# Two loads and one wait moved at the tail of the down projection: the last tile's weights issued before two operand loads, and the residual rows read back without waiting for the last split

## The reference, cut to what matters

```
g_, u_ = split(f @ w_gate_up)                 # (544 x 1024) @ (1024 x 5632)
hid    = silu(g_) * u_                        # 544 x 2816
x      = x + rmsnorm(hid @ w_down, g_ffn_post)  # w_down 2816 x 1024; x here is x1, the residual
```

## Time and profile before

| | us |
|---|---|
| Median of three runs | 766.47 |
| The profiled execution's own time | 765.87 |
| Its span, first to last instruction | 764.1 |
| TensorE busy (matmuls) | 753.5, 99% of the span |
| VectorE busy | 519.1, 68% |
| ScalarE busy | 376.5, 49% |
| GpSimd busy | 124.1, 16% |

### The profile page before, as it was taken

One profiled execution on the slowest core, in us unless ns is written; L12 is line 12 of the kernel. 1 busy time (PEld: TensorE's weight loads), 2 busy tenths in 40 slices (PEclk: granted clock), 3 DMA queues, 4 the chain that ended last, 5 costly groups with the idle time before them and its releaser, 6 DMA issues.

```text
span 764.1 us, 16113 instructions
## 1 busy us (share of the span) xinstructions
PE 753.5 (99%) x5909; PEld 713.0 (93%) x5909; DVE 519.1 (68%) x822; ACT 376.5 (49%) x670; POOL 124.1 (16%) x240
## 2 busy tenths in 40 slices
PE   8999999999999999999999999999999999999995
PEld 6988899898898899987899999999999999999995
DVE  7556838647666565784469887778777899665543
ACT  7334625634634642343456555545555468444441
POOL 6602102010120110012000000000000000373553
PEclk9999999999999999999999999999999999999998
DMA  9545546545554225525470333322333112433273
GB/s 259 167 111 119 152 115 139 154 106 125 136 130 105 73 60 169 165 79 178 158 207 12 111 110 110 107 83 85 110 110 109 56 49 84 136 93 110 71 219 133
DMA packets 183097, 91.77 MB, mean 120 GB/s; under 512 B 50358, under 2 KB 175754, under 8 KB 183052
## 3 DMA queue, kind: packets, MB, share of 16 engines
q1 hardware_dynamic: 176606, 82.41, 39.1%
q0 software_dynamic: 5264, 8.41, 3.9%
q10 hardware_dynamic: 1182, 0.35, 0.2%
HBM read 82.37 MB, written 6.81 MB: 117 GB/s over the span
## 4 chain that ended last, share of the span: by engine, by line
PE 93%; POOL 3%; DMA 2%; DVE 1%; issue 1%; DVEq 0%; SPq 0%; POOLq 0%; ACT 0%
PE ps L1079 34%; PE ps L1468 28%; PE ps L1362 6%; PE ps L1585 6%; PE ps L1570 5%; PE ps L1436 3%; PE ps L1532 2%; PE ps L1285 2%; POOL ytok L646 1%; PE ps L1186 1%; PE ps L1200 1%; PE ps L1218 1%; DMA strow<-in_state_h_dram 1%; PE ps L1260 1%; DVE ytok L2870 1%
## 5 line engine op out<-in xcount | busy, mean ns | idle before, releaser
L1079 PE MATMUL ps<-xin_hi,w_hi 128*128 128x272 f32 x544 | 117.0, 296 | 0.0
L1079 PE MATMUL ps<-xin_hi,w_lo 128*128 128x272 f32 x544 | 112.4, 288 | 0.0
L1079 PE MATMUL ps<-xin_lo,w_hi 128*128 128x272 f32 x544 | 112.2, 288 | 0.0
L2248 DVE TENSOR_TENSOR w_lo<-w_raw,w_hi 128x1024 fp32r<-128x1024 f32 (+1 forms) x47 | 57.1, 1214 | 52.5 <-ACT w_hi L1665 52.2
L1079 PEld LDWEIGHTS ps<-xin_hi,w_hi 128*128 128x128 f32 x544 | 84.8, 188 | 8.1 <-issue 7.6
L646 POOL DMA_DIRECT2D ytok<-yz x56 | 39.4, 710 | 310.9 <-DVE yz L2809 307.2
L1079 PEld LDWEIGHTS ps<-xin_lo,w_hi 128*128 128x128 f32 x544 | 85.4, 188 | 0.0
L1079 PEld LDWEIGHTS ps<-xin_hi,w_lo 128*128 128x128 f32 x544 | 85.0, 189 | 0.0
L1665 ACT ACTIVATE w_hi<-w_raw 128x1024 fp32r<-128x1024 f32 (+1 forms) x48 | 50.0, 1045 | 52.3 <-PE ps L1079 34.6
L1468 PE MATMUL ps<-xq_lo,b_hi 128*128 128x272 f32 x160 | 46.6, 292 | 0.0
L1468 PE MATMUL ps<-xq_hi,a_lo 128*128 128x272 f32 x160 | 46.4, 290 | 0.0
(11 more groups left out here) (394 smaller groups left out, 2137.5 us busy)
## 6 DMA issues: line engine op xcount, KB each, us to landing
w_raw<-in_w_in_dram SPq DMA_DIRECT2D x68, 256.0 KB, 3.4
g_raw<-in_w_gate_up_dram SPq DMA_DIRECT2D x40, 256.0 KB, 3.8
u_raw<-in_w_gate_up_dram SPq DMA_DIRECT2D x20, 256.0 KB, 3.0
e_raw<-in_w_gate_up_dram SPq DMA_DIRECT2D x20, 256.0 KB, 4.2
raw_p<-in_w_down_dram SPq DMA_DIRECT2D x24, 192.0 KB, 2.7
kc<-in_cache_k_dram SPq DMA_DIRECT2D x64, 64.0 KB
vc<-in_cache_v_dram SPq DMA_DIRECT2D x64, 64.0 KB
raw<-in_w_down_dram SPq DMA_DIRECT2D x12, 320.0 KB, 3.2
```

Of the source, the lines that this page charges most:

```text
L1079: mm = e.matmul(ps[:, bank + h, 0:HT], wt[:, kw, :], xt[:, kx, h * HT:h * HT + HT], start=first and wt is wh and xt is xh, stop=last and ( ...
L2248: e.tensor_tensor(wl[:, 0:k, :], w_raw[s][:, 0:k, :], wh[:, 0:k, :].bitcast(F32), ALU.subtract).then_inc(lo_done, count)
```

## The change

Two edits, and one rewrite that changes no instruction. First, SP's issue of the four transfers for `C_LAST` and `C_LAST + 1` moves from behind the last pair's plain loads 6 and 7 to ahead of them; its condition is now the low part of operand 10 (that and the sums of the last pair). Second, GpSimd no longer waits for all 45 low parts before it loads the residual rows of token groups 1 to 3; the wait for TensorE's use of operand 9 stays. The helper `move_y` is moved into the GpSimd program with the same instructions.

```diff
                     load_op(n + 1, "22", raw_22, KB, 2 * n + 4)
                     e.wait_ge(op_l, OP_0 + o + OP_S4 + 1)
                     load_op(n + 1, "12", raw_12, KB, 2 * n + 3)
+                else:
+                    e.wait_ge(op_sum, SUM_0 + 4 * N7)
+                    e.wait_ge(op_l, OP_0 + o + OP_S4 + 1)
+                    for c in range(2):
+                        k0 = sum(DOWN_K[:c])
+                        load(C_LAST + c, (1 + c) % 2, wd[:, k0:k0 + DOWN_K[c], (KD - 1) * P:KD * P], DOWN_K[c])
                 for i in (6, 7):
                     e.wait_ge(op_l, OP_0 + o + OP_P2 + i - 5)
                     load_plain(n, i)
...
-            e.wait_ge(op_sum, SUM_0 + 4 * N7)
-            for c in range(2):
-                k0 = sum(DOWN_K[:c])
-                load(C_LAST + c, (1 + c) % 2, wd[:, k0:k0 + DOWN_K[c], (KD - 1) * P:KD * P], DOWN_K[c])
-
             load(C_LAST + 2, 1, wd[:, KF - DOWN_K[2]:KF, (KD - 1) * P:KD * P], DOWN_K[2])
...
             for m in range(KD - 3):
                 for part in range(3):
-                    move_y(e, m, m % 2, part, y_moved)
+                    move_y(m, m % 2, part)
             e.wait_ge(op_used, OP_0 + OPS7 * (N7 - 1) + OP_S1 + 1)
-            e.wait_ge(op_l, OP_0 + OPS7 * N7)
             for tt in (1, 2, 3):
                 e.dma_start(x1tok[:, tt, :], token_rows(x1_dram, tt)).then_inc(x1_back, 16)
```

More of the change, by code:

```diff
@@ L632, in program @@
         D_PAIR_BANK = 2 * D_PAIR[1]
[L634 to L648, removed]
         block = ctx.enter_context(nc.Block())
@@ L1051, in _, with move_y @@
                 e.wait_ge(x1_out[j], 64 if UNITS[j] == TT else 16)
+            def move_y(m, s, part):
+                tile = bass.ds(m * P, P)
+                prompt = ytok[:, 0:TT, tile].rearrange("p t (d c) -> p t d c", c=BLK)
+                sample = ytok[0:TS, TT, tile].rearrange("p (d c) -> p d c", c=BLK)
+                if part == 0:
+                    e.wait_ge(consts, C_ZERO)
+                    e.wait_ge(y_turned, m + 1)
+                for d in range(P // BLK):
+                    rows = slice(BLK * d, BLK * d + BLK)
+                    if part < 2:
+                        c0 = part * (2 * P + TS)
+                        e.dma_start(prompt[:, 2 * part:2 * part + 2, d, :], yz[s][rows, c0:c0 + 2 * P]).then_inc(y_moved, 16)
+                    else:
+                        e.dma_start(sample[:, d, :], yz[s][rows, 2 * P:2 * P + TS]).then_inc(y_moved, 16)
             for m in range(KD - 3):
                 for part in range(3):
-                    move_y(e, m, m % 2, part, y_moved)
+                    move_y(m, m % 2, part)
             e.wait_ge(op_used, OP_0 + OPS7 * (N7 - 1) + OP_S1 + 1)
-            e.wait_ge(op_l, OP_0 + OPS7 * N7)
             for tt in (1, 2, 3):
@@ L1059, in _ @@
             for part in range(3):
-                move_y(e, KD - 3, 1, part, y_moved)
+                move_y(KD - 3, 1, part)
             e.wait_ge(op_used, OP_0 + OPS7 * N7 - 1)
@@ L1064, in _ @@
             for part in range(3):
-                move_y(e, KD - 2, 0, part, y_moved)
+                move_y(KD - 2, 0, part)
         @block.tensor
```

## The result

The changed kernel takes 773.34 us (median of 6, 771.34 to 773.56), the kernel before 766.62 us beside it (median of 6, 765.87 to 767.20). The ratio is 1.0083, with an interval of 1.0069 to 1.0095: 6.7 us slower. The forecast was 768.6 with a range of 766.4 to 772.0. Its direction holds, its time does not.

The account below looks back on a forecast made before the run. TensorE is busy 99%, but GpSimd's move chain sets the end. With T = 730.5 the first output rows come 2.1 us later: 765.87 + 2.1 = 768.0, or 768.6 against the median 766.47; range 766.4 to 772.0.

Parts of the forecast that it names:

- The step that failed: While load 6 is in SP's queue, the residual loads get 0.4 of the DMA engines: 1.3 us more for load 6.
- SP's edit: Four transfers ahead of load 6 gain nothing and delay its landing from 726.44 to 729.2.
- T: Start of ScalarE's high part of operand 13, behind load 6: 726.58 in the kernel before, forecast 730.5.
- the ends of 729.2 to 734.4: Bounds on T: nothing lost to the residual loads, or SP's queue stopped for their whole stream of 5.2 us.
- second rival: At load 6, engines take turns by piece, SP's queue gets 13%: T 732.9 to 733.7, end 771.0; chance 0.28.
- first rival: Residual loads cost SP's queue nothing, as it was flowing first: T = 729.2, end 767.3; chance 0.18.
- The third: Rival: load 6 hardly late, moves' way shortened; at T 726.6 the median is 764.7; chance 0.12.
- the shortened way of the moves: GpSimd's moves of tile 5 start without residual loads in front and land without their traffic: 1.8 us given back.
- The sum from T on: On the move chain: moves of tile 5 from T + 5.85, first output rows at T + 26.2.
- The stall of TensorE: TensorE waits 0.8 us ahead of operand 13 and 1.2 ahead of operand 14, together T - 728.5.
- The clock: TensorE's granted clock after a gap of over 3 us: unpriced, nothing in the sum, 1 us left in the range.
- The signs to look for: Late operand 13 released by raw_p's DMA, load 6 landing after 4 us or more, two TensorE stalls, chain ending through moves.

Follow-up runs that it names:

- trace with T at 730.38: Kernel before with SP's edit alone and GpSimd's three residual loads issued behind the moves of tile 5: 772.19 us against 766.66, ratio 1.0078.
- first filled one: Changed kernel plus 36 matmuls with unread result ahead of TensorE's wait for operand 13, run by itself: 771.57 us against 766.28 for the kernel before.
- experiments on small pieces: Changed kernel with residual loads described in 512-byte pieces (772.12 us, ratio 1.0087), then cut into two loads each (769.26, ratio 1.0035).
- last experiment: Kernel before, its SP order kept, with the three residual loads issued by SP behind the last tile's four transfers: 765.15 us against 766.44, ratio 0.9987.
- filled kernel: Changed kernel plus 36 matmuls with unread result ahead of operand 13, the second time: 772.17 us against 766.44 for the kernel before.
- filled pair: Changed kernel again (772.94 us) beside it with 36 unread matmuls ahead of operand 13 (772.17), both against 766.44 for the kernel before.

## Why the prediction was wrong, point by point

**The step that failed** is the one that says how two such queues share, put as "I give the residual loads 0.4 of the engines". In the changed kernel they took 69% from 729 to 734, in its repetition and its near copies 68 to 79%, and SP's queue had 14 to 22%. The term was 1.3 us; it measures 735.30 - 729.50 = 5.8 against the run with SP's edit alone (4.9 against the trace with T at 730.38, whose landing took longer). T was put at 730.5 and came at 735.30: 4.8 late, outside even the ends of 729.2 to 734.4. The end was 768.0 for a profiled execution and came at 772.70, 4.7 late. But for 0.3 of drift, the whole miss is this term.

It failed because I averaged two cases, and one of them was misread. From 738.2 to 740 SP's queue held 87%, and I took this as SP's queue holding off the residual loads. But the three residual loads are 1.57 MB, and GpSimd's queue had moved 1.51 MB by 738.2: the stream was nearly over, and the row shows no contest. The one contest among the rows was the other case, one packet of SP's in 5.2 us.

I then chose by who was flowing first. SP's queue was, with 1.08 of the 1.245 MB up to load 6 behind it by 728, and it gave way all the same. The time of the meeting was off too, and to the forecast's advantage: the residual data came at about 728 and not at 726.5, so that 0.17 MB was left and not 0.62, and even this took 7 us. I had a better estimate in the prediction itself: 27 and 183 ns for a piece, 13% for SP's queue.

**The second rival** was right in kind: 13% forecast, 14% seen. It had 0.28 where the forecast had 0.42. It too fell short: T 732.9 to 733.7, 735.3 measured, the end 771.0 for the median, 773.34 measured. Two things lie in the difference. Load 7's 0.2 MB is in the queue as well, and SP's queue moved 0.36 MB from 728 to 736. And the last engines finish alone: the share of SP's queue was still 17.5% in the microsecond from 734 and 9% in the one from 735, with GpSimd's nearly done. How much each is worth was not measured apart.

The Trainium skill, "DMA: Bandwidth & Descriptors", section "Queues, rings and completion order", says that an engine takes turns between queues and drains a whole packet from one before it switches. If a packet of the trace is such a packet, the profiled execution agrees: the packets came out nearly even (374 and 402) and the bytes did not (1.36 and 0.20 MB). The repetition of the same kernel does not (397 and 666), nor do the near copies (384 and 530 in the first filled one), and the experiments on small pieces did not change the packets, so no run here shows that the turn is the cause.

**The first rival** (the residual loads cost nothing) is excluded: it gave T = 729.2, and the earliest T with them in flight beside a load 6 that stands behind the four transfers is 732.20. **The third** (faster) needed T below 728.4; no profiled execution with SP's edit reached it (729.50 and 730.38 were the earliest). Its mechanism, the shortened way of the moves, is real: it is what the last experiment collects with T at 726.39, though it brings 1.3 us and not the 1.8 worked out. There the first output rows come at T + 26.6, not T + 26.2: the rows still flow beside the moves of tile 5, the last of which landed in 2.37 us, not 1.6.

**SP's edit** held, with T = 729.2 for it alone (729.50, with 0.25 of drift; 730.38 with 0.45 in the other trace without residual loads beside load 6). So did the claim that its early transfers gain nothing. What the prediction did not see is that with this edit alone the residual loads, held back by the later T, meet the transfers of `C_LAST + 2` (5.3 us of ScalarE's wait, and TensorE's side only 0.4 from setting the end). In the changed kernel they are long gone by then.

**The sum from T on** held to 0.1 us: T + 5.82 for the moves against T + 5.85, T + 26.11 against T + 26.2. **The stall of TensorE** followed its rule for operand 13: ready at T + 1.17, wanted at 730.89, so 5.6 with T = 735.30; seen 5.1, the later start of this execution (about 0.3) with it. At operand 14 no stall is left: its low part was ready at 739.31 + 0.56 = 739.87, before the slowed TensorE came to it at about 740.7. So the sign that the two stalls add up to T - 728.5, 6.8 here, did not hold. It was the lower clock that took the second one away, for with the clock at 1.00 the filled kernel shows it, near the 1.2 forecast:

```profile
739.77 0.52 PE L1589 MATMUL ps<-hid_hi,op_hi 128*128 128x272 f32 x2 [0.92 <-DVE op_lo L2774]
```

**The clock** fell as feared, to the lower level from about 735.7 to 742.5, and its price was left out of the sum; by the filled pair this was right to 1 us. TensorE's side kept 1.3 of its 2.0 us.

**The signs to look for:** the late high part, the release by the DMA of `raw_p`, the long landing of load 6 and the moves without loads in front all came. The sign that the chain ends through the moves did not come in the chain of waits, for the near coincidence told of above.

**Still open:** what sets the shares of two queues; why the first residual data came 2.7 us after the issue here (2.7 to 3.2 in all six traces in which SP's queue was at about 100% just then, 1.3 in the other five in which GpSimd issues these loads); why SP's edit alone spreads over 5.5 us, and what its slower executions lost.

## What to carry to other kernels

A load that sets the path is best not left to share the engines with a stream of another queue, whoever was first: here it paid to put such traffic into the same queue behind it. Check then that the queue has room. When an edit lets bulk traffic start earlier, or another edit makes it start later, list every small load in flight during its whole stream; each of the two halves here had a victim of its own. Where two rows of a trace give opposite shares, look first whether both streams still had work in each of them. Let the range reach beyond both ends; and here an estimate from the packets' sizes and times came nearer than who came first.

## What the runs showed of the hardware that I had not expected

- In this kernel a queue that was already flowing lost most of the engines to one that started later: 94.7% in 724 to 728, 13.9% in 729 to 734. A 192 KB load landed in 10.0 us instead of 2.2.
- Loads described in 512-byte pieces and issued by GpSimd still moved in packets of 3.4 KB on average (0.61 MB in 180).
- GpSimd's issue of moves stood still for 5.3 and 5.5 us with the residual rows (some 2 MB) ahead in its own queue, and went on 1.2 to 1.3 us after the last of them had landed; in the changed kernel, where the rows had long landed, the gaps at the same place are 1.89 and 0.88 us.
- TensorE's granted clock stood at the 1.2 GHz level from about 735.7 to 742.5, behind a stretch without a matmul from 731.3 to 736.5; in this place it cost about 1 us by the medians and nothing in the traces. The lower clock also hid TensorE's second stall, which the filled kernel shows (0.92 us).
